# Two decoder stacks in float32 on one core: the mixer's first steps in another order, and the latent attention's up-projections as three products of rounded halves

## The chip, the core and the metric

The kernel runs on one core of a Trainium2 chip. Its engines run side by side and wait for each other through semaphores: TensorE (PE, matrix products into PSUM; PEld are its weight loads), VectorE (DVE), ScalarE (ACT, functions from tables that have to be loaded), GpSimd (POOL) and SyncE (SP), which only issues transfers. The metric is the time of one execution on the device in microseconds. Less is better.

## The reference, cut to what matters

Two stacks of two layers each, batch 1, 256 tokens of width 1024, all float32. The first stack's layer is feed-forward, token mixer, feed-forward, each with a layer norm behind it. The second stack has a multi-head latent attention (MLA) and a gated linear attention (GLA), over 256 tokens and 256 context tokens. The change touches the head of the token mixer and the latent attention:

```python
def token_mixer(h, w_in, w_out, gdn_conv, ...):
    qkv_a, a_a, b_a, z_a, qkv_b, qk_c, v_c, i_c, f_c, o_c = jnp.split(h @ w_in, IN_SPLITS, axis=-1)
    qa, ka, va = jnp.split(causal_conv_silu(qkv_a, gdn_conv), 3, axis=-1)
    qa = l2norm(split_heads(qa).astype(f32))
    ka = l2norm(split_heads(ka).astype(f32))
    ...
    beta = jax.nn.sigmoid(b_a.astype(f32))
    oa = gated_delta_rule(qa, ka, va, g.transpose(0, 2, 1), beta.transpose(0, 2, 1)).transpose(0, 2, 1, 3)
    ...

def mla_mixer(hc, hx, row, col, w_in, q_norm_g, w_uq, kv_norm_g, w_ukv, w_out):
    def project(h, rotate):
        cq, ckv, kr, gate = split_last(h @ w_in, (MLA_Q_RANK, MLA_KV_RANK, MLA_ROPE, MLA_WIDTH))
        q = (rms_norm(cq, q_norm_g) @ w_uq).reshape(b, n, MLA_HEADS, MLA_NOPE + MLA_ROPE)
        kv = (rms_norm(ckv, kv_norm_g) @ w_ukv).reshape(b, n, MLA_HEADS, MLA_NOPE + MLA_V)
        ...
    ox = attention_blocks(qx, jnp.concatenate([kc, kx], axis=1), jnp.concatenate([vc, vx], axis=1))
```

MLA has 16 heads, the ranks are 384 for queries and 256 for keys and values, a head has 64 + 32 columns of query and key and 64 of value.

## The kernel before

**Products of halves.** A float32 product on TensorE is two instructions. Most large products are done otherwise: an operand x is split into hi, x rounded to the shorter format fp32r, and lo, x - hi, and a product is the sum of hi·hi, lo·hi and hi·lo, one instruction each. ScalarE writes the hi part of a weight chunk (a copy with a rounding), VectorE the lo part (a subtraction, below called a low).

**The ring.** All weights come from one stream of chunks of 128 x 2048 float32 (1 MB), which SyncE loads in order into 8 ring slots. A chunk may be loaded when the chunk 8 places before it is released. For most chunks of halves the hi part takes the next slot and the lo part is written over the chunk (`take_both`).

**The order of work** on each engine is the order in which the program is written; there is no scheduler. A mixer (`mixer(l)`, m = 1 and 4) begins with six projections on TensorE, chunks 12, 0, 1, 2, 3, 4 of `w_in` (`WIN_FIRST`), into PSUM banks 1 to 6. Chunk 12 gives a gate tile (tile 24, ScalarE, `gate_or_copy`) and the rows of decays (`r_u`, VectorE). Chunks 0 to 4 give tiles 0 to 8 of queries, keys and values of the delta rule, each through `conv` on VectorE (four instructions) and SiLU on ScalarE, and gate tile 9. After the fifth projection TensorE needs the squares of tiles 0 to 5 (`l2sq`) for the sums `blk` x `g_sq`, six float32 products (`wk,tab`, twelve instructions), then goes on with the sixth projection, with fills (`fill(n)` takes the next items of a list of independent work, `BESIDE`: products p6.0, p6.1, p7.0, ...), with the transposed rows, the products key x key and key x query (`kk`, `qk`), and p13. VectorE does between these the lows of the chunks to come (`win_low`), `rows()` (running sums of decays), the normalised queries and keys, `g_kb` and `g_vb` (keys and values times beta), the mask on the decays (`gb_read`) and low 8.

In the layer norm ahead of a mixer ScalarE writes the normed tokens also into `res` (`affine(..., "normed")`, eight instructions), VectorE waits for these before the mixer, and also for ScalarE's reading of the gate tile (`proj_read_a`).

**The latent attention** (`mla()`, m = 6). The input stage makes 14 units of 128 columns from 7 chunks `mla_in`; units 0 to 4 are the latents `cq` (3 tiles of queries' and 2 of keys' latents, 512 tokens wide), which are normalised on VectorE once their sums are there (`cqr`, `cqn`). Between the last units stand `keys_values(0, 0..3)` and `queries(0)`, `queries(1)`. The sixteen heads follow. In head h TensorE does `scores(h)`, `turned(h-1)` (12 transposes), `queries(h+2)`, in even heads `weighted(h//2-1)`, and below head 12 `keys_values(h//4+1, h%4)`. VectorE does `maxima(h)` (L2594, L2595), the copy of part of the turned scores, in heads 12 to 14 a low of the output weights, `normalise(h)`, a copy of half the keys where h%4 < 2, `q_part(h+2)` (rotation of the query), `out_part` in even heads and `heads_low` in odd ones. ScalarE does the exponentials of `h` between maxima and normalise, and copies. `queries` and `keys_values` are plain float32 products on `cq`: 48 of 512 columns for the queries; 16 of 512 and 32 of 256 for keys and values. Their weights are 4 chunks `uq` (4 heads each) and 2 chunks `ukv` (8 heads each). VectorE also computes the modulation vectors of GLA there (`mod_part`, `LATE_MODS`), two halves of a chunk each.

Of the kernel before, what the change touches and what calls it, by code (L numbers as in the profile page):

```python
# [10 lines left out]
F32 = mybir.dt.float32  # L11
# [79 lines left out]
def build(nc, stream, cond_in, cols_in, tab_in, wg_in, xt_in, ct_in, out, spread, marks):  # L91
# [3 lines left out]
    with ExitStack() as ctx:  # L95
# [22 lines left out]
        assert nc.sbuf_base == wk_at + 4 * WK  # L118
        cond = sb("cond", [P, D])
        mod = sb("mod", [P, 4, 48])  # L120
# [10 lines left out]
        x2lo = nc.alloc_sbuf_tensor_at("x2lo", [P, KT, 2 * T], F32R, offset=wk_at + 4 * NEW)  # L131
# [98 lines left out]
        r_u, r_ab, r_ln = [g_at[:, 256 * i:256 * i + 256] for i in range(3)]  # L230
# [62 lines left out]

        def tree_bank(li):

            return 7 if li % 2 == 0 else 6
# [6 lines left out]
        LATE_AT = {2: (0,), 3: (1, 2), 4: (3, 4), 5: (5,), 6: (6, 7)}  # L303
# [37 lines left out]
        def _(eng):  # L341
# [156 lines left out]
            def mixer(l):  # L498
# [140 lines left out]
                for i, ch in enumerate(WIN_FIRST):  # L639
# [19 lines left out]
                for p in range(3, 6):  # L659
                    eng.wait_ge(*step_of("proj_read", m, p))  # L660
# [6 lines left out]
                eng.wait_ge(vector_done, step("kb", m))  # L667
                eng.wait_ge(vector_done, step("gb_read", m))
# [10 lines left out]
                eng.wait_ge(scalar_done, step("ekd", m))  # L679
# [158 lines left out]
            def mla():  # L838
# [51 lines left out]
                def keys_values(g, i):  # L890

                    w, b = state["ukv"], bank(6)
                    if i < 2:
                        for k in range(2):
                            at = 256 * (g % 2) + P * i
                            mm(b, w[:, k, at:at + P], cq[:, 3 + k, :], k == 0, k == 1)
                    else:
                        for t in range(2):
                            for k in range(2):
                                at = P * (2 * i - 4 + t)  # L900
                                mm(b[:, 256 * t:256 * t + 256], cq[:, 3 + k, at:at + P], w[:, k, 512 + 256 * (g % 2):768 + 256 * (g % 2)], k == 0, k == 1)
                    if g % 2 and i == 3:
# [7 lines left out]
                def next_keys(j):  # L910

                    state["ukv"] = tiles(take("ukv", j), D)
                    state["ukv_no"] = held[0]
# [7 lines left out]
                def queries(h):  # L921

                    if h % 4 == 0:
                        state["uq"] = take("uq", h // 4)[:, 0:1536].rearrange("p (k n) -> p k n", k=3)
                        state["uq_no"] = held[0]
                    w, hh = state["uq"], h % 4
                    if h == 0:
                        eng.wait_ge(*step_of("in2_read", m, 8))
                    elif h == 1:
                        eng.wait_ge(*step_of("in2_read", m, 12))  # L930
                    else:
                        eng.wait_ge(vector_done, step("q_read", h - 1))
                    for k in range(3):
                        mm(bank(0 if h else 2), w[:, k, P * hh:P * hh + P], cq[:, k, :], k == 0, k == 2)
                    if hh == 3:
# [92 lines left out]
                for i in range(3, 7):  # L1028
# [4 lines left out]
                    if i == 5:  # L1033
                        next_keys(0)
                    for n in (2 * i, 2 * i + 1):
# [15 lines left out]
                        if n >= 10:  # L1051
                            if n == 10:
                                eng.wait_ge(scalar_done, step("cqe", 1))
                                eng.wait_ge(vector_done, step("cqn", m))
# [39 lines left out]
                for h in range(MLA_H + 1):  # L1094
# [17 lines left out]
                    if h < 12:  # L1112
                        if h == 4:
                            next_keys(1)
# [339 lines left out]
        def _(eng):  # L1454
# [90 lines left out]
            def norm(m):  # L1545
# [34 lines left out]
                for c in range(2, 4):  # L1580
                    if to_ffn:
                        whole(m + 1, c)
                    else:
                        win_high(m + 1, c)
                g0_, b0_ = COLS["ln_g"][0] + 8 * m, COLS["ln_b"][0] + 8 * m
                affine(m, res[:, :, XS], tiles(ff_cen, 256), cols[:, g0_:g0_ + 8], cols[:, b0_:b0_ + 8], range(0, 4))
                eng.wait_ge(vector_done, step("xn", m, 3))
# [1433 lines left out]
```

## Time and profile before

| | us |
|---|---|
| median of three runs | 1775.43 |
| lowest, highest | 1773.72, 1776.09 |
| the profiled execution | 1776.33 |
| its span | 1774.3 |
| TensorE busy | 1686.1 |
| VectorE busy | 1323.5 |
| ScalarE busy | 777.0 |

The profile is of one execution. The span runs from the first to the last instruction. A busy TensorE is not one at its peak, since its instructions overlap: the time that a product costs is the distance from one start to the next, not the duration of one. Idle time of an engine counts only where others wait for it.

### The profile page before, as it was taken

The page shows a single profiled execution, that of the slowest core. Times are in us where ns is not written, and L with a number is a line of the kernel's source. Part 1 is how long each engine was busy: PE and PEld are TensorE (multiplying, and loading weights), DVE is VectorE, ACT ScalarE, POOL GpSimd, SP SyncE. Part 2 cuts the span into 40 slices and gives each one's busy share as a digit, 9 for nine tenths or more (in the row PEclk, how much of TensorE's full clock was granted, in tenths as well). Part 3 has the DMA queues.
Part 4 walks back from the last instruction along what each step waited for, and adds up shares of the span by engine and source line. Part 5 has one row for each costly group of instructions (what it writes and reads, how often), then busy time and mean ns, then how long its engine had stood idle before and what let it go on. Part 6 is the DMA issues. An engine that isn't in the chain of part 4 may idle for free. (4 is left out here: it accounts for less than half of the span.)

```text
span 1774.3 us, 30736 instructions
## 1 busy us (share of the span) xinstructions
PE 1686.1 (95%) x13112; PEld 1512.1 (85%) x13112; DVE 1323.5 (75%) x1965; ACT 777.0 (44%) x997; POOL 6.3 (0%) x14
## 2 busy tenths in 40 slices
PE   2999989999999999999899999999999999999998
PEld 2999978888899989999798779999886555759898
DVE  7777788855877778998878557999767768567844
ACT  2433365323633354343753327343652345355354
POOL 0000000000000000000000000000000000000000
PEclk9999999999999999999999999999999999999999
DMA  9868536351577746885364435776153200223102
GB/s 390 340 270 305 207 108 246 133 202 63 203 305 285 282 180 271 321 316 198 119 227 155 179 128 207 273 279 229 48 213 143 95 34 15 107 95 143 48 24 96
DMA packets 48807, 331.92 MB, mean 187 GB/s; under 512 B 5256, under 2 KB 8480, under 8 KB 9376
## 3 DMA queue, kind: packets, MB, share of 16 engines
q1 hardware_dynamic: 47808, 326.79, 48.2%
q0 software_dynamic: 864, 3.17, 0.7%
q8 instruction: 104, 1.70, 0.4%
q14 instruction: 31, 0.25, 0.0%
HBM read 328.87 MB, written 1.07 MB: 186 GB/s over the span
## 5 line engine op out<-in xcount | busy, mean ns | idle before, releaser
L347 PE MATMUL ps<-xhi,low 128*128 128x256 f32 x2048 | 499.5, 283 | 4.2 <-ACT xhi L1459 4.2
L347 PEld LDWEIGHTS ps<-xhi,low 128*128 128x128 f32 x2048 | 360.5, 190 | 6.4 <-ACT xhi L1459 5.6
L347 PE MATMUL ps<-xhi,whi_wk 128*128 128x256 f32 x1072 | 298.5, 288 | 40.5 <-ACT xhi L1459 38.7
L347 PE MATMUL ps<-xlo,whi_wk 128*128 128x256 f32 x1072 | 291.5, 281 | 0.0
L1459 ACT ACTIVATE wk<-ps 128x256 f32<-128x256 f32 (+5 forms) x219 | 108.1, 503 | 386.8 <-PE ps L347 320.8
L1459 ACT ACTIVATE whi_wk<-ring 128x2048 fp32r<-128x2048 f32 x100 | 191.6, 1918 | 195.3 <-DMA ring<-in_stream_dram 145.2
L347 PEld LDWEIGHTS ps<-xhi,whi_wk 128*128 128x128 f32 x1072 | 203.5, 195 | 43.2 <-issue 41.8
L2068 DVE TENSOR_TENSOR low<-ring,whi_wk 128x2048 fp32r<-128x2048 f32 (+1 forms) x101 | 228.4, 2264 | 6.6 <-ACT whi_wk L1459 6.6
L347 PE MATMUL ps<-wk 64*64 64x64 f32 (+10 forms) x2712 | 210.3, 262 | 5.8 <-ACT wk L1459 4.3
L347 PEld LDWEIGHTS ps<-wk 64*64 64x64 f32 (+4 forms) x2712 | 162.3, 146 | 55.0 <-issue 29.5
L347 PEld LDWEIGHTS ps<-xlo,whi_wk 128*128 128x128 f32 x1072 | 197.9, 189 | 0.0
L347 PE MATMUL ps<-hhi,low 128*128 128x256 f32 x704 | 196.8, 280 | 0.0
L2083 DVE CUSTOM_DVE_ANT_0 ring<-ring,cond,cols 128x1024 f32<-128x1024 f32 x144 | 178.3, 1278 | 11.0 <-DMA cols<-in_cols_dram 10.9
L1459 ACT ACTIVATE wk<-wk 128x256 f32<-128x256 f32 (+9 forms) x154 | 94.6, 643 | 200.9 <-DVE wk L2074 154.9
L347 PE MATMUL ps<-xa,ring 128*128 128x256 f32 (+1 forms) x608 | 146.0, 396 | 3.4 <-DVE xa L2071 3.1
L2068 DVE TENSOR_TENSOR wk<-wk,ps 128x256 f32<-128x256 f32 (+2 forms) x130 | 57.9, 462 | 122.1 <-ACT wk L1459 108.6
L347 PE MATMUL ps<-hhi,whi_wk 128*128 128x256 f32 x528 | 148.0, 280 | 0.0
L347 PE MATMUL ps<-hlo,whi_wk 128*128 128x256 f32 x528 | 147.9, 280 | 0.0
L347 PEld LDWEIGHTS ps<-xa,ring 128*128 128x128 f32 x608 | 114.3, 191 | 30.1 <-issue 11.5
L347 PEld LDWEIGHTS ps<-hhi,low 128*128 128x128 f32 x704 | 132.2, 188 | 0.0
L2068 DVE TENSOR_TENSOR low<-ring,low 128x2048 fp32r<-128x2048 f32 x41 | 93.2, 2286 | 48.4 <-ACT low L1459 48.2
L347 PE MATMUL ps<-wk,tab 128*128 128x256 f32 (+3 forms) x370 | 96.6, 422 | 22.8 <-ACT wk L1459 19.9
(141 smaller groups left out, 2861.7 us busy)
## 6 DMA issues: line engine op xcount, KB each, us to landing
ring<-in_stream_dram SPq DMA_DIRECT2D x302, 1024.0 KB, 5.7
ring<-in_cond_dram SPq DMA_DIRECT2D x4, 1024.0 KB, 4.6
wk<-spread_dram POOLq DMA_DIRECT2D x4, 384.0 KB, 5.1
wk<-spread_dram POOLq DMA_DIRECT2D x2, 768.0 KB, 6.9
tab<-in_tab_dram SPq DMA_DIRECT2D x1, 1440.0 KB, 20.5
res<-in_xt_dram SPq DMA_DIRECT2D x1, 1024.0 KB, 17.5
res<-in_ct_dram SPq DMA_DIRECT2D x1, 1024.0 KB, 9.9
out_dram<-wk SPq DMA_DIRECT2D x4, 256.0 KB, 2.4
```

Source lines behind the costliest of these rows:

```text
L347: last[0] = nc.tensor.matmul(o, l, r, start=start, stop=stop, skip_group_check=free)
L1459: return nc.scalar.activation(o, i, f, **kw)
L2068: return do(v.tensor_tensor(o, a, b, op), *key)
L2083: return do(v.tensor_tensor_reduce(o, w, c, 1.0, bias, MUL, ADD, total), *key)
```

## The change

**In the mixers.** ScalarE no longer writes `res` in the layer norm ahead of a mixer but in two halves inside it, behind SiLU of tiles 1 and 3, and reads the gate tile of chunk 12 only after the exponentials and logarithm of the rows. VectorE waits for neither. Low 5 moves from behind tiles 2 and 3 to behind tile 5, ahead of `rows()`. Tile 8's convolution moves from before low 7 to behind `g_kb`; `kk` on TensorE and the decays on ScalarE then wait for `g_kb` only, and `kk` no longer for the mask on the decays. The two fills on ScalarE stand apart. `r_u` and its neighbours have other places in memory.

**In the latent attention.** `queries` and `keys_values` become three products of halves each. The latents are split once: five roundings on ScalarE (`cqh`), five lows on VectorE (`cql`), and one of them is copied later (`cqh_later`). The weights come in 8 chunks of 768 columns (2 heads each) and 4 of 1024 (4 heads each), each in a whole ring load; both halves stay in its slot (`half_places`), rounded by `up_high` and subtracted by `up_low`. One modulation vector moves behind the last chunk `mla_in` (`LATE_AT`).

In the diff a line of "..." marks what is left out.

```diff
@@ tables
-        LATE_AT = {2: (0,), 3: (1, 2), 4: (3, 4), 5: (5,), 6: (6, 7)}
+        LATE_AT = {2: (0,), 3: (1, 2), 4: (3,), 5: (4,), 6: (5, 6, 7)}
+        UP_SIZE = {"uq": 768, "ukv": 1024}
+        def half_places(n, size):
+            return low[:, n % RING, D:D + size], low[:, n % RING, 0:size]
@@ TensorE, mixer
+                        eng.wait_ge(scalar_done, step("proj_read_a", m, 0))
                         eng.wait_ge(scalar_done, step("l2sq", m))
...
-                for p in range(3, 6):
-                    eng.wait_ge(*step_of("proj_read", m, p))
...
-                eng.wait_ge(vector_done, step("kb", m))
-                eng.wait_ge(vector_done, step("gb_read", m))
+                eng.wait_ge(vector_done, step("kbk", m))
...
-                eng.wait_ge(scalar_done, step("ekd", m))
+                for p in range(3, 6):
+                    eng.wait_ge(*step_of("proj_read", m, p))
+                eng.wait_ge(scalar_done, step("proj_read_a", m, 5))
@@ TensorE, latent attention
                         for k in range(2):
-                            mm(b, w[:, k, at:at + P], cq[:, 3 + k, :], k == 0, k == 1)
+                            mm(b, hi[:, k, at], cq_hi(3 + k), k == 0, False)
+                            mm(b, lo[:, k, at], cq_hi(3 + k), False, False)
+                            mm(b, hi[:, k, at], cq_lo[:, 3 + k, :], False, k == 1)
...
+                def up_halves(kind, i, n):
+                    take(kind, i)
+                    eng.wait_ge(vector_done, step("ulow", kind, i))
+                    return [tiles(p, n) for p in half_places(held[0], UP_SIZE[kind])]
...
                     for k in range(3):
-                        mm(bank(0 if h else 2), w[:, k, P * hh:P * hh + P], cq[:, k, :], k == 0, k == 2)
+                        mm(o, hi[:, k, at], cq_hi(k, h), k == 0, False)
+                        mm(o, lo[:, k, at], cq_hi(k, h), False, False)
+                        mm(o, hi[:, k, at], cq_lo[:, k, :], False, k == 2)
...
-                        if h == 4:
-                            next_keys(1)
+                        if h % 4 == 0:
+                            next_keys(h // 4 + 1)
@@ ScalarE, mixer
-                eng.wait_ge(tensor_done, step("proj", m, 0))
-                gate_or_copy(24, bank(1, 0, 256), "proj_read_a", m, 0)
...
                 win_high(m, 4)
+                eng.wait_ge(vector_done, step("proj_read", m, 0))
+                gate_or_copy(24, bank(1, 0, 256), "proj_read_a", m, 0)
                 for t in range(6):
                     silu(t)
-                    if t == 1:
-                        win_high(m, 5)
-                    if t == 3:
-                        win_high(m, 6)
+                    if t in (1, 3):
+                        win_high(m, 5 + t // 2)
+                        normed(m - 1, t // 2)
@@ ScalarE, latent attention
                 root(rs2, "cqr", m)
+                for t in (3, 4, 0, 1, 2):
+                    eng.wait_ge(vector_done, step("cqn", t))
+                    act(cq_hi(t), cq[:, t], ACT.Copy, "cqh", t).then_inc(scalar_done, 1)
...
+                        up_high(("ukv", "uq")[(n - 7) // 2], 0)
...
+                up_high("uq", 1)
+                up_high("ukv", 1)
...
+                    if h % 2 and h < 12:
+                        up_high("uq", h // 2 + 2)
+                    if h in (2, 6):
+                        up_high("ukv", h // 4 + 2)
@@ VectorE, norm and mixer
-                eng.wait_ge(scalar_done, step("normed", m))
+                if m % 3:
+                    eng.wait_ge(scalar_done, step("normed", m))
...
-                    if ch in (12, 4):
-                        eng.wait_ge(scalar_done, step("proj_read_a", m, i))
...
-                    if ch < 2:
-                        win_low(m, 4 + ch)
+                    if ch == 0:
+                        win_low(m, 4)
                     if ch == 2:
+                        win_low(m, 5)
                         rows()
                         win_low(m, 6)
...
+                tt(g_kb, qkv[:, 3:6], tiles(g_pair[:, 0:768], 256), MUL, "kbk", m).then_inc(vector_done, 1)
+                eng.wait_ge(scalar_done, step("proj_read_a", m, 5))
+                conv(8, bank(6, 0, 256), "proj_read", m, 5)
@@ VectorE, latent attention
+                eng.wait_ge(vector_done, done.count)
+                for t in (3, 4, 0, 1, 2):
+                    eng.wait_ge(scalar_done, step("cqh", t))
+                    tt(cq_lo[:, t], cq[:, t], cq_hi(t).bitcast(F32), SUB, "cql", t).then_inc(vector_done, 1)
+                def up_low(kind, i):
+                    n, size = found["chunk_no", kind, i][1], UP_SIZE[kind]
+                    hi, lo = half_places(n, size)
+                    eng.wait_ge(scalar_done, step("uround", kind, i))
+                    tt(lo, ring[:, n % RING, 0:size], hi.bitcast(F32), SUB, "ulow", kind, i).then_inc(vector_done, 1)
...
+                up_low("uq", 1)
                 q_part(1)
+                copy(cqh_later[:, :], cqh_first[:, :].bitcast(F32), "cqh_later").then_inc(vector_done, 1)
+                up_low("ukv", 1)
                 modulation(7)
...
+                    if h % 2 and h < 12:
+                        up_low("uq", h // 2 + 2)
+                    if h in (2, 6):
+                        up_low("ukv", h // 4 + 2)
```

Where the rows come to stand, at three places. First ScalarE at the start of the first mixer, before the change, from the roundings of chunks 2 and 3 (`low<-ring`) on; `res<-wk,cols` are the eight writes, `res<-ps` is the gate tile:

```order
L1459 ACTIVATE low<-ring 128x2048 x2
L1459 ACTIVATE res<-wk,cols 128x256 x8
L1459 ACT_TABLE_LOAD
L1459 ACTIVATE res<-ps 128x256
L1459 ACT_TABLE_LOAD
L1459 ACTIVATE wk<-wk 128x256
L1459 ACTIVATE wk<-wk 32x256
L1459 ACTIVATE small<-cols 128x1
L1459 ACT_TABLE_LOAD
L1459 ACTIVATE wk<-wk 128x256
L1459 ACTIVATE low<-ring 128x2048
L1459 ACT_TABLE_LOAD
```

And after it:

```order
L1491 ACTIVATE low<-ring 128x2048 x2
L1491 ACTIVATE wk<-wk 128x256
L1491 ACTIVATE wk<-wk 32x256
L1491 ACTIVATE small<-cols 128x1
L1491 ACTIVATE wk<-wk 128x256
L1491 ACTIVATE low<-ring 128x2048
L1491 ACT_TABLE_LOAD
L1491 ACTIVATE res<-ps 128x256
L1491 ACT_TABLE_LOAD
L1491 ACTIVATE wk<-wk 128x256 x2
L1491 ACTIVATE low<-ring 128x2048
L1491 ACTIVATE res<-wk,cols 128x256 x4
```

The eight writes have moved in two halves behind later roundings (the second half comes four rows further on), the gate tile behind the rows' functions, and two of four table loads are gone.

Second, VectorE in the first mixer, from the end of tile 3's convolution to the first row of the row work (`wk<-wk 128x256`); a convolution is a TENSOR_SCALAR and three rows behind it, `low<-ring,low` is the low of a weight chunk. Before:

```order
L2074 SCALAR_TENSOR_TENSOR wk<-ps,cols,wk 128x254
L2074 SCALAR_TENSOR_TENSOR wk<-ps,cols,wk 128x253
L2068 TENSOR_TENSOR low<-ring,low 128x2048
L2071 TENSOR_SCALAR wk<-ps,cols 128x256
L2074 SCALAR_TENSOR_TENSOR wk<-ps,cols,wk 128x255
L2074 SCALAR_TENSOR_TENSOR wk<-ps,cols,wk 128x254
L2074 SCALAR_TENSOR_TENSOR wk<-ps,cols,wk 128x253
L2071 TENSOR_SCALAR wk<-ps,cols 128x256
L2074 SCALAR_TENSOR_TENSOR wk<-ps,cols,wk 128x255
L2074 SCALAR_TENSOR_TENSOR wk<-ps,cols,wk 128x254
L2074 SCALAR_TENSOR_TENSOR wk<-ps,cols,wk 128x253
L2074 SCALAR_TENSOR_TENSOR wk<-wk 128x256
```

After:

```order
L2129 SCALAR_TENSOR_TENSOR wk<-ps,cols,wk 128x254
L2129 SCALAR_TENSOR_TENSOR wk<-ps,cols,wk 128x253
L2126 TENSOR_SCALAR wk<-ps,cols 128x256
L2129 SCALAR_TENSOR_TENSOR wk<-ps,cols,wk 128x255
L2129 SCALAR_TENSOR_TENSOR wk<-ps,cols,wk 128x254
L2129 SCALAR_TENSOR_TENSOR wk<-ps,cols,wk 128x253
L2126 TENSOR_SCALAR wk<-ps,cols 128x256
L2129 SCALAR_TENSOR_TENSOR wk<-ps,cols,wk 128x255
L2129 SCALAR_TENSOR_TENSOR wk<-ps,cols,wk 128x254
L2129 SCALAR_TENSOR_TENSOR wk<-ps,cols,wk 128x253
L2123 TENSOR_TENSOR low<-ring,low 128x2048
L2129 SCALAR_TENSOR_TENSOR wk<-wk 128x256
```

Low 5 stood ahead of the convolutions of tiles 4 and 5 and now stands behind them, ahead of the row work.

Third, VectorE in head 3 of the latent attention, from the copy of the turned scores to the maxima of head 4 (`whi_xa<-xa,o_hi` is `heads_low`). Before:

```order
L2077 COPY wk<-ps 128x512
L2603 RECIPROCAL small<-small 128x4
L2071 TENSOR_SCALAR wk<-wk,small 128x256 x2
L2071 TENSOR_SCALAR wk<-wk,small 128x512 x2
L2068 TENSOR_TENSOR wk<-ps,tab 96x512
L2068 TENSOR_TENSOR tab<-ps,tab 32x512
L2068 TENSOR_TENSOR wk<-wk,tab 32x512
L2068 TENSOR_TENSOR whi_xa<-xa,o_hi 128x512
L2594 TENSOR_REDUCE small<-ps 128x2
```

After:

```order
L2132 COPY wk<-ps 128x512
L2674 RECIPROCAL small<-small 128x4
L2126 TENSOR_SCALAR wk<-wk,small 128x256 x2
L2126 TENSOR_SCALAR wk<-wk,small 128x512 x2
L2123 TENSOR_TENSOR wk<-ps,tab 96x512
L2123 TENSOR_TENSOR tab<-ps,tab 32x512
L2123 TENSOR_TENSOR wk<-wk,tab 32x512
L2123 TENSOR_TENSOR whi_xa<-xa,o_hi 128x512
L2123 TENSOR_TENSOR low<-ring,low 128x768
L2665 TENSOR_REDUCE small<-ps 128x2
```

There is one row more, the low of a `uq` chunk, ahead of the next head's maxima. So it is in every odd head below 12; heads 2 and 6 get one of 128x1024 (`ukv`) in the same place.

## Rows read from the trace of the kernel before

**Rows 1.** The page, part 1: busy time and share of the span.
```profile
PE 1686.1 (95%) x13112; PEld 1512.1 (85%) x13112; DVE 1323.5 (75%) x1965; ACT 777.0 (44%) x997; POOL 6.3 (0%) x14
```

**Rows 2.** Windows: length, busy PE, PEld, DVE, ACT, POOL; granted clock, DMA share, GB/s.
```profile
262.00:270.00 8.00, 2.76 (x20) 2.50 (x19) 7.32 (x18) 4.18 (x5) 0.00 (x0) 0.85 0.46 156
270.00:275.00 5.00, 5.00 (x16) 4.01 (x15) 4.80 (x7) 0.74 (x2) 0.70 (x2) 0.55 0.01 3
```

**Rows 3.** Timeline, PE: start, duration, instruction [idle before <-releaser]; the two mixers.
```profile
269.32 5.38 PE L347 MATMUL ps<-wk,tab 128*128 128x256 f32 x12 [5.24 <-ACT wk L1459]
...
297.72 0.51 PE L347 MATMUL ps<-low,xhi 128*128 128x256 f32 x2
...
303.37 0.80 PE L347 MATMUL ps<-tab,wk 64*64 64x64 f32 x20
...
883.48 2.05 PE L347 MATMUL ps<-wk,tab 128*128 128x256 f32 x4 [5.24 <-ACT wk L1459]
```

**Rows 4.** Timeline, DVE, first mixer.
```profile
246.76 0.54 DVE L2071 TENSOR_SCALAR wk<-ps,cols 128x256 f32<-128x256 f32 x1 [3.64 <-ACT res L1459]
...
263.11 0.48 DVE L2071 TENSOR_SCALAR wk<-ps,cols 128x256 f32<-128x256 f32 x1
...
267.32 0.43 DVE L2074 SCALAR_TENSOR_TENSOR wk<-wk 128x256 f32<-128x256 f32 x1
...
274.03 2.29 DVE L2068 TENSOR_TENSOR low<-ring,low 128x2048 fp32r<-128x2048 f32 x1
...
283.35 2.28 DVE L2068 TENSOR_TENSOR low<-ring,low 128x2048 fp32r<-128x2048 f32 x1
...
294.05 2.29 DVE L2068 TENSOR_TENSOR low<-ring,low 128x2048 fp32r<-128x2048 f32 x1
```

**Rows 5.** Timeline, ACT, start of the first mixer.
```profile
240.90 4.03 ACT L1459 ACTIVATE res<-wk,cols 128x256 f32<-128x256 f32 x8
244.95 1.28 ACT L1459 ACT_TABLE_LOAD   x1
```

**Rows 6.** Timeline, PE, end of the latent attention's input stage.
```profile
...
1360.04 0.62 PE L347 MATMUL ps<-whi_xa,low 128*128 128x512 f32 x2
...
1360.74 0.63 PE L347 MATMUL ps<-whi_xa,low 128*128 128x512 f32 x2
...
1361.43 1.89 PE L347 MATMUL ps<-ring,wk 128*128 128x256 f32 x8
1363.16 2.74 PE L347 MATMUL ps<-wk,ring 128*128 128x512 f32 x6
1365.73 2.75 PE L347 MATMUL ps<-wk 96*128 96x256 f32 x8
```

**Rows 7.** Timeline, DVE, attention heads: scores' first maximum (L2594) of heads 4 to 8.
```profile
1406.36 0.69 DVE L2594 TENSOR_REDUCE small<-ps 128x2 f32<-128x512 f32 x1
...
1414.06 0.69 DVE L2077 COPY wk<-ps 64x512 f32<-64x512 f32 x1 [1.62 <-PE ps L347]
...
1417.65 0.68 DVE L2594 TENSOR_REDUCE small<-ps 128x2 f32<-128x512 f32 x1
...
1437.75 0.69 DVE L2594 TENSOR_REDUCE small<-ps 128x2 f32<-128x512 f32 x1 [1.23 <-PE ps L347]
...
1447.00 0.69 DVE L2594 TENSOR_REDUCE small<-ps 128x2 f32<-128x512 f32 x1
```

**Rows 8.** Timeline, DVE: two subtractions of 1024 columns, two products of 768.
```profile
1284.91 2.36 DVE L2068 TENSOR_TENSOR x2lo<-wk,whi_xa 128x1024 fp32r<-128x1024 f32 x2
...
288.01 1.82 DVE L2068 TENSOR_TENSOR wk<-wk 128x768 f32<-128x768 f32 x2
```

**Rows 9.** Timeline, PE, head 4: the weighted sum.
```profile
1409.29 2.81 PE L347 MATMUL ps<-wk 128*64 128x256 f32 x24
```

**Rows 10.** Timeline, DVE, just before the heads.
```profile
1365.93 0.69 DVE L2068 TENSOR_TENSOR wk<-ps,tab 96x512 f32<-96x512 f32 x1 [2.70 <-PE ps L347]
```

**Rows 11.** DMA issues of 235 to 290 us: KB each, median us to landing.
```profile
ring<-in_stream_dram SPq DMA_DIRECT2D x9, 1024.0 KB, 4.8
```

More of the change, by code:

```diff
@@ L229, in build @@
         g_t, g_tt, g_dt, g_at, g_att = [W(SCR + 1536 * i, 1536) for i in range(5)]
-        r_u, r_ab, r_ln = [g_at[:, 256 * i:256 * i + 256] for i in range(3)]
+        r_u, r_ab, r_ln = W(23040, 256), W(23296, 256), r_rw
         g_sq = g_t
@@ L292, in build, with cq_hi @@
         a_end, a_tot = small[:, 40:44], small[:, 44:48]
+        def cq_hi(t, h=0):
+            return cqh_q[:, t] if t < 2 else cqh_kv[:, t - 3] if t > 2 else cqh_later[:, :] if h > 1 else cqh_first[:, :]
+        def half_places(n, size):
+            return low[:, n % RING, D:D + size], low[:, n % RING, 0:size]
         def tree_bank(li):
@@ L1053, in mla @@
                                 eng.wait_ge(scalar_done, step("cqe", 1))
-                                eng.wait_ge(vector_done, step("cqn", m))
+                                eng.wait_ge(vector_done, step("cql", 4))
+                                next_keys(0)
                             else:
@@ L1584, in norm, with normed @@
                         win_high(m + 1, c)
+                if to_ffn:
+                    normed(m, 0)
+                    normed(m, 1)
+            def normed(m, part):
                 g0_, b0_ = COLS["ln_g"][0] + 8 * m, COLS["ln_b"][0] + 8 * m
-                affine(m, res[:, :, XS], tiles(ff_cen, 256), cols[:, g0_:g0_ + 8], cols[:, b0_:b0_ + 8], range(0, 4))
-                eng.wait_ge(vector_done, step("xn", m, 3))
-                affine(m, res[:, :, XS], tiles(ff_cen, 256), cols[:, g0_:g0_ + 8], cols[:, b0_:b0_ + 8], range(4, 8), "normed", m)
+                if part:
+                    eng.wait_ge(vector_done, step("xn", m, 3))
+                affine(m, res[:, :, XS], tiles(ff_cen, 256), cols[:, g0_:g0_ + 8], cols[:, b0_:b0_ + 8], range(4 * part, 4 * part + 4),
+                       *(("normed", m) if part else ()))
             def ffn(l, f):
@@ L1711, in mixer @@
                 gate_or_copy(9, bank(6, 256, 512), "proj_read_a", m, 5)
+                fill(1)
                 silu(6)
                 silu(7)
+                fill(1)
+                win_high(m, 8)
                 silu(8)
-                win_high(m, 8)
-                fill(2)
                 eng.wait_ge(pairs_in, 32 * (l + 1))
-                eng.wait_ge(vector_done, step("kb", m))
+                eng.wait_ge(vector_done, step("kbk", m))
                 cs = tiles(g_pair[:, 768:1536], 256)
@@ L1874, in mla, with up_high @@
                     act(tiles(sq2, 512)[:, t], res[:, t, :], ACT.Square, "sq7", t).then_inc(scalar_done, 1)
+            def up_high(kind, i):
+                n, size = found["chunk_no", kind, i][1], UP_SIZE[kind]
+                eng.wait_ge(landed[n % RING], loads(n))
+                act(half_places(n, size)[0], ring[:, n % RING, 0:size], ACT.Copy, "uround", kind, i).then_inc(scalar_done, 1)
             def high(*tag):
@@ L2971, in chunk_of @@
     if kind == "ukv":
-        heads = range(8 * tag[1], 8 * tag[1] + 8)
+        heads = range(4 * tag[1], 4 * tag[1] + 4)
         return columns(a["mla_w_ukv_2"][0], [(128 * h, 64) for h in heads] + [(128 * h + 64, 64) for h in heads], 2)
@@ L2975, in chunk_of @@
         s = []
-        for h in range(4 * tag[1], 4 * tag[1] + 4):
+        for h in range(2 * tag[1], 2 * tag[1] + 2):
             s += [(96 * h, 96)] + [(96 * h + 64 + p, 8) for p in [8, 0, 24, 16]]
```

54 lines of the change are left out of this document (34 added, 20 removed).

## The prediction

> **What bounds the kernel now.** I read the page's busy shares first, then TensorE's idle times in the timeline, then, at each of them, the engine it waits for. TensorE is busy 95% of the span [rows 1], so only two things can shorten the program: TensorE's waits, and TensorE's work where nothing else sets the pace. The longest wait of a mixer is the one before the sums of squares (`wk,tab` x12): 5.24 us, in both mixers [rows 3]. It costs more than itself. In the window with it the granted clock falls, and in the next five microseconds it is 0.55 of full, half speed (1.2 GHz) for nearly all of it [rows 2]; the twelve sums take 4.9 us from 269.32 to 274.22, about twice the 2.45 of full speed. From there to the end of the mixer TensorE has no wait of 0.3 us: fills cover it.
>
> In the 16 attention heads it is different. From head to head I follow VectorE's first maximum (L2594). Heads 4 to 7 take 40.64 us [rows 7], and in them VectorE idles 1.62 and 1.23 us on TensorE; else it waits only for the exponentials, some 1.9 us a head, which follow its own maxima. So a chain through VectorE and ScalarE sets the pace of most heads, and TensorE that of a few.
>
> **The mixers, step by step** (the first; the second is built alike). TensorE ends its fifth projection at 264.1 (269.32 - 5.24). One projection is 48 products of halves; 48 of them take 303.37 - 297.72 = 5.65 us [rows 3], 0.118 each. What comes last before the sums is VectorE's sixth convolution, done at 267.3 [rows 4]. Its chain stood still for 3.64 us before 246.76, waiting for ScalarE: eight writes of `res` (4.03 us) and a table load (1.28) stood in front of the gate that VectorE waited for [rows 4, 5]. The change takes both out of VectorE's way: it begins at 243.1 (246.76 - 3.64), and from then on it is the projections that hold it. The fourth ends at 258.4, two convolutions take 267.32 - 263.11 = 4.2 [rows 4], so the sixth ends at 262.6: 4.7 earlier. SiLU and squares took 2.0 from there to the sums, so these begin near 264.7. The writes of `res` return in two halves of 2.0 us between ScalarE's SiLUs; by 4.8-us landings [rows 11] and 1.9-us roundings ScalarE too reaches the squares only at 262.9, so they just fit. TensorE waits 0.6 instead of 5.24, keeps its clock, and is done with the sums at 267.2 instead of 274.2: 7.0 ahead. `res` itself is read again only at the mixer's end, so its later writing holds up nobody.
>
> Not all of it stays. The next weights' lows are VectorE's, and that gained only 4.7. One low of 2.3 us now stands ahead of the row work, which begins at 264.9 and takes 274.03 - 267.32 = 6.7 [rows 4]; low 6 ends at 273.9. TensorE, with its sixth projection, is there at 272.9: a wait of 1.0. Low 7 follows two convolutions instead of three and ends at 280.4, TensorE comes at 279.9: 0.5. Then keys, 5.85 us of small products, and low 8. In the old trace low 8 ended at 296.34, 10.7 after low 7; the ninth convolution (2.1) has moved into this stretch, less a wait of 0.9 that it can fill: 292.3 to 293.2, I take 293.0. TensorE gets there at 292.0, so its next product begins at 293.0 against 297.72 [rows 3]: 4.7 earlier. Behind it, masks and decays on VectorE are 3.3 earlier and had 1.5 us of slack, which just covers the rest. Two mixers: **9.4 us less**, with 6 and 13 as ends (another 1.7 us lost on each; or nearly the whole 7.0 kept).
>
> **The latent attention.** TensorE's own saving is plain. A float32 product of 512 columns is two instructions of (1365.73 - 1363.16)/6 = 0.43 us, one of 256 two of (1363.16 - 1361.43)/8 = 0.216; three products of halves of 512 columns take 1360.74 - 1360.04 = 0.70 [rows 6], of 256 columns 0.353 [rows 3]. There are 64 and 32 of them: 128 x 0.43 + 64 x 0.216 = 68.8 us before, 64 x 0.70 + 32 x 0.353 = 56.1 after, 12.7 less. For that VectorE gets 5 lows of 512 columns, 8 of 768 and 4 of 1024 and a copy; ScalarE the roundings, which fit its idle time. The prices: 2.36/2 = 1.18 for 1024, 1.82/2 = 0.91 for 768 [rows 8].
>
> Of the loads, SyncE issues six more of 1 MB each (12 chunks of latent weights for 6), in a stretch where the queue stands idle for most of the time; their ring slots come free a head or more ahead of the roundings, but for one. Ahead of the heads TensorE gains 2.2 us: two queries of 0.47 less, four parts of keys and values of 0.33 less. VectorE had 2.70 us of idle time there [rows 10] and 4 more ahead of low 5, where the five new lows of the latents go. What remains on it after that are 1.18 + 0.91 + 0.91 + 1.18 us of weights' lows and 0.7 of the copy, 4.9, of which the idle times and an earlier landing of the last input weights take nearly all but the last. That last one, the low of key weights 1, is bound in another way: its ring slot comes free with the first group's values at 1361.4, 4.8 to landing [rows 11], 1.0 to round, 1.2 for the low, and the first maximum stands behind it on VectorE: 1369.1 against 1368.6. Cost **+0.5** (0 to +3).
>
> In the heads I take each by its kind. An odd head below 12 has the chain maxima, exponentials, scaling, query, low of the heads, and no wait on TensorE; a low of 768 columns comes behind it, in front of the next head's maxima: 0.91 and 0.05 of gap, six times, +5.8. What TensorE saves there hides nothing, since it already waited. In an even head the weighted sum starts 2.93 us behind the maxima (1409.29 - 1406.36 [rows 7, 9]), for VectorE's copy of the turned scores, so shorter queries don't move it; behind it the shorter keys give 0.33 in heads 4 and 8 (where VectorE waited 1.62 for them) and 0.43 in head 10. Heads 2 and 6 had 1.23 us of slack on VectorE and get a low of 1.18, +0.1 each. Heads 12 and 13 were set by VectorE's lows of the output weights and stay. Sum: 5.8 - 0.66 - 0.43 + 0.2 = **+4.9**. The part that was to gain 12.7 us loses 5.4. Its ends: -9 if TensorE's path counted after all, +9 if the lows cost VectorE their full price everywhere.
>
> The sum is -9.4 + 5.4 = -4.0 us. The profiled execution took 1776.33 us (span 1774.3 and 2.0 around it), so 1772.3; the median of the three runs is 0.9 lower, so 1771.4.
>
> One rule of the skill speaks against part of this. In the trace the table load takes 1.28 us and the next function follows at once [rows 5]. The Trainium skill (ScalarE: Activation LUTs, What ACT_TABLE_LOAD costs) puts 1.38 us of draining beside the load. With its figure the two loads ahead of the first SiLU would put ScalarE behind VectorE by some 2 us, each mixer would gain 3.4 instead of 4.7, and the sum would be -1.4; I go by the row.
>
> **Rivals.** (a) *TensorE sets the pace in the heads.* Its 95% speaks for it, the missing VectorE idle time in odd heads against. Whole: -9.4 - 12.7, 1753; in part, with the lows in time that VectorE idles anyway and the attention at no change: 1766. (b) *The mixer's wait only changes its name.* ScalarE's path to the squares ties with VectorE's; if a landing takes 7 us or the moved writes come in its way, TensorE waits 2.5 us more, and each mixer gains 2 to 2.5: -4.7 + 5.4, 1776. (c) *The half clock in the heads, slower.* TensorE's work per head falls from 9.6 to 8.8 us while the head gets longer, so it idles more often, up to 1.5 us at a time. If the clock falls as it did behind the mixer's wait, each fall costs up to 2.45 us [rows 3]; four falls turn the sum, six give +14.7 - 4.0, 1786. Against it: TensorE's idle times there stay well below 5.24. The Trainium skill (TensorE: Matmul & The Clock Gate, A second HAM failure mode: psum-queue depth-cycling) tells of a kernel whose clock swings between its two levels from frequent short idles alone; no run here shows that yet. (d) *The weights' lows come late ahead of the heads*, the first maximum by 3 us more and PE's queries behind them: 1775.
>
> **Chances.** Forecast 0.45 (own range 1768 to 1775); (a) 0.25, most of it near 1766; (b) 0.15; (c) 0.07; (d) 0.08. Range: 1761 to 1779, which leaves out (a) whole and (c). 0.2% is 3.6 us, about what a measurement of this kernel can tell from none. Faster by more: four fifths of the forecast and (a), 0.61; within: the rest of the forecast, most of (b) and of (d), 0.26; slower: (c) and what is left of (b) and (d), 0.13.
>
> **What would show it.** The mixers: TensorE's idle time before `wk,tab` x12 under 1.5 us and the clock at 1.00 behind it; instead waits near 1, 0.4 and 1 us for lows 6, 7 and 8; the first product of `low,xhi` in the first mixer at 293. The attention: from head 0's first maximum to head 12's 124 us instead of 119; VectorE without idle time on TensorE in odd heads, TensorE's waits on `low` from VectorE. I am wrong if the heads get shorter, if the clock in them is below 0.98, or if the squares on ScalarE start after 264.

## The result, and the profile after

| | us |
|---|---|
| before, median of four runs | 1774.78 |
| changed, median of four runs (1783.34 to 1786.53) | 1784.39 |
| ratio, 95% interval | 1.0057 (1.0045 to 1.0069) |
| changed, measured again (e12) | 1.0043 (1.0029 to 1.0056) |
| predicted | 1771.4 (1761 to 1779) |

The change made the kernel slower by 8 to 10 us; a gain of 4 was predicted. I follow TensorE through the changed kernel's trace, which is of the slowest of its four executions (1786.53 us). First its timeline in the two mixers (start, duration, instruction, idle before and releaser), which answers to [rows 3]:

```profile
264.73 2.83 PE L363 MATMUL ps<-wk,tab 128*128 128x256 f32 x12 [0.62 <-ACT wk L1491]
...
273.98 0.51 PE L363 MATMUL ps<-xhi,low 128*128 128x256 f32 x2 [0.78 <-DVE low L2123]
...
280.48 0.48 PE L363 MATMUL ps<-xhi,low 128*128 128x256 f32 x2 [0.35 <-DVE low L2123]
...
286.52 5.92 PE L363 MATMUL ps<-wk 64*128 64x128 f32 x48
295.66 0.77 PE L363 MATMUL ps<-low,xhi 128*128 128x256 f32 x2 [3.22 <-ACT wk L1491]
...
304.01 1.61 PE L363 MATMUL ps<-tab,wk 64*64 64x64 f32 x48
...
902.16 10.77 PE L363 MATMUL ps<-wk 64*128 64x128 f32 x48 [2.31 <-DVE wk L2123]
912.86 0.79 PE L363 MATMUL ps<-low,xhi 128*128 128x256 f32 x2
...
920.04 1.61 PE L363 MATMUL ps<-tab,wk 64*64 64x64 f32 x48
```

The wait before the sums went from 5.24 to 0.62 us, and the waits for lows 6 and 7 are the small ones forecast. TensorE is as far ahead as it should be until the keys' products. Then comes a wait that was not forecast: 3.22 us behind the keys' products in the first mixer, 2.31 ahead of them in the second. The windows of the changed kernel (length, busy times, granted clock, DMA share, GB/s) show what it drags along:

```profile
262.00:270.00 8.00, 7.38 (x53) 6.90 (x53) 7.47 (x17) 5.81 (x6) 0.00 (x0) 1.00 0.44 163
270.00:275.00 5.00, 4.22 (x36) 4.02 (x35) 4.83 (x4) 4.13 (x4) 1.75 (x3) 1.00 0.16 29
...
292.00:300.00 8.00, 4.78 (x24) 4.62 (x24) 7.70 (x10) 3.83 (x14) 0.00 (x0) 0.66 0.53 219
...
905.00:915.00 10.00, 9.88 (x47) 9.28 (x47) 9.63 (x11) 6.46 (x19) 0.00 (x0) 0.50 0.55 228
```

The clock of 0.85 and 0.55 around the sums [rows 2] is 1.00 now, but it falls to half speed (1.2 GHz) behind the new wait. In the second mixer the 48 small products take 10.70 us from start to start where they took 5.85. VectorE's timeline says who is late, in the first mixer and in the second:

```profile
285.43 0.17 DVE L2132 COPY small<-wk 128x3 f32<-128x3 f32 x1 [2.71 <-DMA wk<-spread_dram]
...
293.23 2.28 DVE L2123 TENSOR_TENSOR low<-ring,low 128x2048 fp32r<-128x2048 f32 x1
...
901.08 0.17 DVE L2132 COPY small<-wk 128x3 f32<-128x3 f32 x1 [4.87 <-DMA wk<-spread_dram]
...
908.88 2.29 DVE L2123 TENSOR_TENSOR low<-ring,low 128x2048 fp32r<-128x2048 f32 x1
```

VectorE stands 2.71 us until the spread rows (`g_pair`, loaded by GpSimd's queue) have landed, 4.87 in the second mixer, and low 8, for which TensorE waits, ends at 295.51 instead of near 293 (911.17 in the second). TensorE's row at 295.66 names ScalarE as the releaser: the last of twelve exponentials there ends within 0.1 us of low 8. But by the program this product waits for low 8 and for a copy of ScalarE that was done at 292.03. Why the rows are late is in the timelines of SyncE's and GpSimd's queues. The kernel before:

```profile
280.38 0.81 SPq L1432 DMA_DIRECT2D ring<-in_stream_dram  x2
...
276.83 1.35 POOL L2850 DMA_DIRECT2D wk<-spread_dram  x2 [1.34 <-DMA spread_dram<-wk]
```

The changed kernel:

```profile
273.24 0.80 SPq L1464 DMA_DIRECT2D ring<-in_stream_dram  x2
...
274.43 1.35 POOL L2928 DMA_DIRECT2D wk<-spread_dram  x2 [1.34 <-DMA spread_dram<-wk]
```

The DMA issues of 264 to 300 us (KB each, median us to landing), before:

```profile
wk<-spread_dram POOLq DMA_DIRECT2D x2, 384.0 KB, 5.1
wk<-spread_dram POOLq DMA_DIRECT2D x1, 768.0 KB, 6.9
```

and changed:

```profile
wk<-spread_dram POOLq DMA_DIRECT2D x2, 384.0 KB, 9.7
wk<-spread_dram POOLq DMA_DIRECT2D x1, 768.0 KB, 13.7
```

Two weight loads of 1 MB leave when the sixth projection has freed their slots. TensorE reaches that 7.1 us earlier; the rows, which hang on VectorE, leave only 2.4 earlier. So the order is reversed: the rows left 3.5 us ahead of the weights and now leave 1.2 us behind them. The DMA queues of the changed kernel in steps of two microseconds (packets, MB, share of the 16 engines' time; q1 carries weights, q0 rows), in turn from 275, 277 and 281 us:

```profile
q1 hardware_dynamic: 94, 0.77, 93.9%
...
q1 hardware_dynamic: 114, 0.80, 95.5%
q0 software_dynamic: 5, 0.02, 2.5%
...
q0 software_dynamic: 119, 0.42, 100.1%
```

Until 279 the weights have the engines nearly to themselves; then the rows pass, at half the weights' rate (0.42 MB in 2 us against 0.80).

In the heads, VectorE's first maxima of heads 0 and 12, which answer to [rows 7]:

```profile
1372.38 0.69 DVE L2665 TENSOR_REDUCE small<-ps 128x2 f32<-128x512 f32 x1
...
1496.92 0.69 DVE L2665 TENSOR_REDUCE small<-ps 128x2 f32<-128x512 f32 x1
```

TensorE in heads 0 and 2:

```profile
1376.94 5.46 PE L363 MATMUL ps<-wk 96*128 96x256 f32 x8 [3.27 <-ACT wk L1491]
...
1393.33 0.70 PE L363 MATMUL ps<-cqh_q,low 128*128 128x512 f32 x2 [1.46 <-DVE low L2123]
```

From head 0 to 12 it is 124.5 us (119.1 before; 124 was forecast). TensorE is 0.6 us behind before at the end of the first mixer, 2.7 at the start of the attention and 9.3 at its end. So in this execution the mixers cost 2.7 instead of giving 9.4, and the attention cost 6.6 instead of 5.4.

### The profile page after: what moved, and what is told of

It reads as the page before. It is cut to its first block and busy times, and to the rows that moved or that the text cites. A ratio compares the mean times of both kernels' runs of the same rounds, so it can differ in the third digit from the quotient of the medians.

```text
span 1783.6 us, 30974 instructions
## 1 busy us (share of the span) xinstructions
PE 1682.8 (94%) x13208; PEld 1530.7 (86%) x13208; DVE 1338.4 (75%) x1983; ACT 785.2 (44%) x1010; POOL 6.3 (0%) x14
## 5 line engine op out<-in xcount | busy, mean ns | idle before, releaser
L363 PE MATMUL ps<-wk 64*64 64x64 f32 (+10 forms) x2712 | 218.0, 266 | 13.5 <-ACT wk L1491 10.0
L363 PEld LDWEIGHTS ps<-wk 64*64 64x64 f32 (+4 forms) x2712 | 167.4, 149 | 59.0 <-issue 31.3
L2123 DVE TENSOR_TENSOR low<-ring,low 128x2048 fp32r<-128x2048 f32 (+2 forms) x53 | 105.6, 2004 | 44.1 <-ACT low L1491 43.9
L363 PE MATMUL ps<-whi_xa,low 128*128 128x256 f32 (+1 forms) x552 | 115.1, 332 | 1.9 <-ACT whi_xa L1491 1.9
## 6 DMA issues: line engine op xcount, KB each, us to landing
wk<-spread_dram POOLq DMA_DIRECT2D x4, 384.0 KB, 10.3
```

The costliest lines, as they stand in the source:

```text
L363: last[0] = nc.tensor.matmul(o, l, r, start=start, stop=stop, skip_group_check=free)
L2123: return do(v.tensor_tensor(o, a, b, op), *key)
```

## The experiments

All ratios are to the kernel before on the same chip, with 95% intervals; 0.001 is 1.8 us. e1 to e4 and e12 ran on one chip, e5 to e11 on another.

**e1, e2, e12: the parts.** e1 has the hunks in the mixers and layer norms alone, e2 all others, e12 is the changed kernel.

> The kernel before with the mixers' part of the change alone. Theory 1 (collision): in the changed kernel two loads of weights leave SyncE's queue at 273.24, 1.2 us ahead of the loads of the spread rows (274.43), where before they left at 280.38, 3.5 us behind them; the rows land late, VectorE stands 2.71 us, TensorE 3.22 us, and the clock falls behind that. Then this kernel is slower than before by about the 2.7 us that the changed kernel is behind at the start of the latent attention: 1777 to 1778. Rival (the prediction's sum holds for the mixers and the loss lies in the interplay with the attention): 1765, faster by 9.4.

> The kernel before with the latent attention's part alone. By the two traces the attention costs 6.6 us (from 2.7 behind at its start to 9.3 at its end): 1781.4. The prediction's sum gave 5.4: 1780.2. If the parts aren't additive (the attention's loads or clock suffer from the mixers), 1775 or less.

> The changed kernel once more, in as many rounds as its parts. The parts alone gave ratios of 1.0006 (mixers) and 1.0032 (attention), together 1.0038; the change gave 1.0057 in fewer runs. If the parts are independent, this comes out near 1.004 (7 us); if they make each other worse (more falls of the clock, or the longer run of loads), near 1.0057 again (10 us).

Measured: e1 1.0006 (0.9997 to 1.0015), e2 1.0032 (1.0020 to 1.0045), e12 1.0043 (1.0029 to 1.0056). The parts add up to 1.0038, inside e12's interval; the first measurement of the change (1.0057, 1.0045 to 1.0069) lies above it. The mixers' part alone is worth nothing, neither the 9.4 of the sum nor clearly a loss, and e1's trace has nearly the waits of the changed kernel's (2.79 and 2.05 us, where that has 3.22 and 2.31). The attention costs 5.7.

**e3, e5, e9: rows first.** SyncE holds back the two loads until the mixer's rows are there; nothing else changes (`hold` lists the first load of each mixer into a slot that the sixth projection frees). e3 is the changed kernel with it, e5 the mixers' part, e9 the kernel before.

```diff
                 if n >= RING:
                     eng.wait_ge(*step_of("chunk", n - RING))
+                for l in range(DEPTH):
+                    if n == hold[l]:
+                        eng.wait_ge(pairs_in, 32 * (l + 1))
```

> The changed kernel, but SyncE waits, before the two loads of weights that the sixth projection frees, until the spread rows of that mixer have landed. Theory 1: rows land in 5 to 7 us as before, VectorE's wait of 2.71 is gone, TensorE's 3.22 and 2.31 too, low,xhi begins near 293.0 and the clock stays up: each mixer gets its 4.7 us, together 12.1 from 1784.4: 1772.3. Rival 2 (the rows are late for another reason, or the order of VectorE's work, keys ahead of the ninth convolution and low 8 last, sets the end anyway): low,xhi stays at 295 or later, 1780 to 1785. Rival 3 (the loads held back come late themselves): new waits for ring in the mixers, over 1785.

> The mixers' part alone (e1), with SyncE waiting for the spread rows as in e3. e3 made the mixers worth about 8.7 us with the attention's part in place (1782.3 of e2 less 1773.65). If collision and attention are independent: ratio to before near 0.995, 1767.8. If the attention's part hid something of it: 1771 or more.

> A control: the kernel before with nothing but SyncE's wait for the spread rows. In its trace the rows' loads leave 3.5 us ahead of the weights' and land before VectorE wants them (285.1 against 287.9). Theory 1: there is no collision to take away, so nothing changes: within 2 us of before. Rival (the wait helps a mixer in itself, or the weights' loads held back come late): more than 3 us faster or slower.

Measured: e3 0.9983 (0.9972 to 0.9993), e5 0.9942 (0.9928 to 0.9956), e9 1.0003 (0.9995 to 1.0012). The DMA issues of e3's first mixer:

```profile
wk<-spread_dram POOLq DMA_DIRECT2D x2, 384.0 KB, 5.8
wk<-spread_dram POOLq DMA_DIRECT2D x1, 768.0 KB, 7.5
```

Its timeline, VectorE's copy and TensorE's next product:

```profile
281.98 0.16 DVE L2137 COPY small<-wk 128x3 f32<-128x3 f32 x1
...
292.20 0.47 PE L363 MATMUL ps<-low,xhi 128*128 128x256 f32 x2 [0.64 <-ACT wk L1496]
```

VectorE waits no more, TensorE 0.64 instead of 3.22. One wait on SyncE's queue is worth 0.0060 in the changed kernel (against e12) and 0.0064 in the mixers' part, 11 us for two mixers, and nothing in the kernel before, where rows left first anyway. So it does not help in itself; it takes back the collision that the change made. Its rivals 2 and 3 fall: the new order of VectorE's work is no hindrance, and the weights held back come in time. With it the mixers' part alone gains 10.3 us, near the 9.4 of the prediction.

**e8: a weaker hold.** The same edit with `rows_stored` in place of `pairs_in`, so that both kinds of load leave together.

> As e3, but SyncE waits only until the rows are stored, so that its two loads of weights leave at the same time as the loads of the spread rows. Theory 1a (what counts is which is queued first at the DMA engines): the rows have 1.35 us of issuing on GpSimd's queue, and the first load of 1 MB still gets ahead of part of them: landings 7 to 9 us, part of the gain, 1776 to 1779. Theory 1b (bandwidth is shared, order doesn't matter): landings of 9 to 10 us as in the changed kernel, 1783. If 5 to 7 us as in e3: 1773.7.

Measured: 1.0051 (1.0039 to 1.0063), no better than the change. The queues' timeline in its first mixer:

```profile
272.72 0.80 SPq L1469 DMA_DIRECT2D ring<-in_stream_dram  x2
...
272.92 1.35 POOL L2933 DMA_DIRECT2D wk<-spread_dram  x2 [1.35 <-DMA spread_dram<-wk]
```

Its DMA issues there:

```profile
wk<-spread_dram POOLq DMA_DIRECT2D x2, 384.0 KB, 10.4
wk<-spread_dram POOLq DMA_DIRECT2D x1, 768.0 KB, 15.9
```

The wait held the weights back by 1.0 us: they leave 9.5 us behind the start of the sums, 8.5 in the changed kernel. They are still 0.2 us ahead of the rows, for which GpSimd's queue needs 1.35 us to issue. So a lead of 0.2 us instead of 1.2 brought the rows' landing nothing (10.4 and 15.9 against 9.7 and 13.7). The result lies near 1b's forecast (9 to 10 us, 1783) and misses 1a's (7 to 9 us, 1776 to 1779). That order doesn't matter at all is not shown by it: in e3 it did, and no kernel here let the rows go first by a fraction of a microsecond. What e8 shows is that leaving together is not enough. The Trainium skill (DMA: Bandwidth & Descriptors, Queues, rings and completion order) says that each DMA engine goes round the queues that have work, a packet at a time. The changed kernel's trace shows sharing only from 279 on (75% and 34% of the time in 279 to 281); in the two microseconds before, the rows' queue had 2.5%.

**e10: the wait and the clock apart.** The changed kernel, rows late, but TensorE fills its waits with products that nobody reads (in the second mixer also six of the keys' products again).

```diff
                 fill(2)
+                for i in range(12):
+                    mm(bank(2, 0, 256), blk, tiles(g_sq, 256)[:, i % 6], True, True)
                 eng.wait_ge(vector_done, step("kbk", m))
...
```

> The changed kernel, rows late as they are, but TensorE fills its waits with products that nobody reads: twelve sums of squares again ahead of the keys' products (about 2.8 us), and in the second mixer six of the keys' products again (1.5 us). This parts the late rows' cost into the wait and the half clock behind it. Theory: the clock stays at full speed from 290 to 303 and from 903 to 916, the first product of low,xhi comes when the last low allows (295.5; about 911), and the clock's share of 2.7 us in the first mixer and 3.1 in the second comes back: 5 to 6 us faster than the changed kernel, near 1780 where that has 1785 to 1786 and before 1776.5. Rival (the clock doesn't hang on the wait, or the filling itself costs): no faster than the changed kernel.

Measured: 1.0027 (1.0018 to 1.0037), against 1.0043 of e12. Windows in both mixers:

```profile
290.00:296.00 6.00, 5.89 (x50) 5.28 (x49) 5.80 (x8) 4.04 (x14) 0.00 (x0) 1.00 0.78 322
...
905.00:912.00 7.00, 6.89 (x61) 6.38 (x60) 6.80 (x8) 4.66 (x17) 0.00 (x0) 1.00 0.64 265
```

In the first mixer TensorE's filling (x24 is twelve float32 products), the first product of `low,xhi`, and VectorE's low 8:

```profile
284.83 5.34 PE L363 MATMUL ps<-wk,tab 128*128 128x256 f32 x24
...
295.96 0.51 PE L363 MATMUL ps<-low,xhi 128*128 128x256 f32 x2
...
291.45 2.29 DVE L2126 TENSOR_TENSOR low<-ring,low 128x2048 fp32r<-128x2048 f32 x1
```

The clock stayed up in both places. But the run does not part the wait from the clock as it was meant to. Its filling was planned at 2.8 us and takes 5.3, so TensorE comes too late for low 8: low 8 ends at 293.74 and the product starts at 295.96, 2.2 us behind it; in the second mixer it is 2.0 (911.38 against 909.36). In time, e10 is 0.0016 below e12, 2.8 us, less than the 5 to 6 expected; the intervals overlap and leave anything from none to nearly 6.

The traces part the two better. In the first mixer low 8 ends 31.4 us behind the end of the fifth projection in the changed kernel, 31.0 in e10, and 28.6 in e5: the lateness itself costs 2.8 us there. In the second mixer it is 33.6 in the changed kernel and again 28.6 in e5, 5.0 us. The clock comes on top of it (see below).

**e4, e11: the attention's lows elsewhere.** e4 is e2 with the lows of the weights behind the maxima, where VectorE waits for the exponentials, and their roundings a head earlier. e11 also puts the low of key weights 1 from ahead of the loop behind the first maxima (the lines with `h == 0`; the hunk of ScalarE is left out).

```diff
-                up_low("ukv", 1)
...
                     if h < MLA_H:
                         maxima(h)
+                    if h == 0:
+                        up_low("ukv", 1)
                     if h:
                         pt_copy(h - 1)
+                    if h % 2 and h < 12:
+                        up_low("uq", h // 2 + 2)
+                    if h in (2, 6):
+                        up_low("ukv", h // 4 + 2)
                     if 12 <= h < 15:
                         out_low(h - 12)
...
                         heads_low((h - 3) // 2)
-                    if h % 2 and h < 12:
-                        up_low("uq", h // 2 + 2)
-                    if h in (2, 6):
-                        up_low("ukv", h // 4 + 2)
```

> The attention's part alone as in e2, but the lows of the query and key weights stand behind the maxima of a head, where VectorE waits 1.8 to 2.6 us for the exponentials, and their roundings on ScalarE a head earlier. Theory (VectorE's and ScalarE's chain sets the pace of the heads, and a low costs only where it stands in the chain): six odd heads lose 0.96 each and TensorE's waits of 1.3 to 2.1 for low are gone: 1781.4 - 5.8 = 1775.6, at best 1 to 2 less since the shorter products now count in the even heads. Rival (the roundings or the landings now come in the way, or TensorE's clock is what costs): 1780 to 1783.

> The attention's part alone with lows behind the maxima and the key weights' low behind the first maxima: is it worth having without the mixers? e7 less e5 says 4.6 us faster than before; e4 (2.4 slower) less the 3 to 4 that the clock kept in the first heads gave in e7's sum says 1 to 2 faster. In the trace, heads 0 to 12 at 117.5 us instead of 119.1, no fall of the clock in 1370 to 1380.

Measured: e4 1.0007 (0.9998 to 1.0016), 4.4 us better than e2 where 5.8 was expected; e11 0.9985 (0.9976 to 0.9993), faster than before. Heads 0 to 12 take 124.5 us in e2, 119.2 in e4, 117.5 in e11. The same lows cost 5.3 us more behind the heads' last step than behind the maxima, where heads 0 to 12 take what they took before: VectorE's place in the chain, not its busy time, was the price. What e4 does not get rid of stands in its last heads:

```profile
1502.47 4.51 PE L363 MATMUL ps<-wk 96*128 96x256 f32 x8 [1.89 <-ACT wk L1491]
```

A wait of 1.89 us, and half speed behind it (4.51 for eight products that take 2.8); in the kernel before the clock is 1.00 there.

**e6, e7: everything together.** e6 is e3 with e4's edit, e7 with e11's too.

> Both remedies on the changed kernel: rows first (e3) and lows behind the maxima (e4). If their gains add, 3.4 us below e3: 1770.2, still 2.4 above e5, which has no attention part. If the clock falls again in the last heads as in e4 (a wait of 1.89 us and half speed behind it), no more than that; if it doesn't, 1768.5.

> e6, and the low of the second key weights stands behind the first head's maxima instead of ahead of them. Ahead of them it costs VectorE 0.8 of waiting for ScalarE (a late landing) and 1.23 of work, and TensorE then waits 3.2 us for the first exponentials and runs at half speed behind that (the next eight products take 5.46 instead of 2.8 us). Theory: first maxima 2.0 earlier, TensorE's wait split and the clock kept: 3 to 4 below e6, 1766.5. Rival: the wait only moves to the keys that need this low, and the clock falls there: 1770.

Measured: e6 0.9948 (0.9937 to 0.9960), e7 0.9915 (0.9903 to 0.9927): 15 us faster than before, the best of all. TensorE at head 0 in e6:

```profile
1360.45 5.46 PE L363 MATMUL ps<-wk 96*128 96x256 f32 x8 [3.20 <-ACT wk L1496]
```

In e7 TensorE waits instead where the program needs the low of key weights 1:

```profile
1357.76 0.70 PE L363 MATMUL ps<-cqh_kv,low 128*128 128x512 f32 x2 [1.21 <-issue]
```

The window of 1360 to 1365 in e6:

```profile
1360.00:1365.00 5.00, 4.55 (x8) 2.67 (x9) 4.34 (x9) 1.50 (x4) 0.00 (x0) 0.50 1.02 424
```

and in e7:

```profile
1360.00:1365.00 5.00, 4.66 (x24) 3.17 (x23) 4.74 (x8) 1.78 (x3) 0.00 (x0) 1.00 1.02 431
```

One wait of 3.20 has become 1.21, the clock stays up, and head 0 takes 9.1 us again instead of 10.1. By the ratios the step is worth 5.9 us, by the two traces 2.6; a part of it is that e6's executions differ among themselves (below).

## Why the prediction was wrong

**The mixers, as far as low 7: right.** A wait of 0.6 was forecast (0.62 and 0.61), sums done at 267.2 (267.21), clock kept there, waits of 1.0 and 0.5 for lows 6 and 7 (0.78 and 0.35), the squares in time. In the changed trace, too, the next function starts 0.02 us behind a table load. The 1.38 us of draining that the Trainium skill puts beside a load (ScalarE: Activation LUTs, What ACT_TABLE_LOAD costs), which by the prediction's estimate would have cost each mixer 1.3, did not show.

**The step that failed** is "low 8 ... I take 293.0" and, with it, "TensorE gets there at 292.0, so its next product begins at 293.0". The working counted VectorE's own instructions and left out that one of them needs the rows from GpSimd's queue. In the old trace the two loads that VectorE's copy at 287.94 waits for landed near 282.6 (the second left about 277.5, 5.1 to landing), and the third at 285.1, so no row showed a wait. I moved VectorE's demand 5 us forward and TensorE's release of two ring slots 7, and let the rows keep pace without looking at what lay ahead of them. Without the collision the step is right: 28.9 us from the fifth projection to that product were forecast, e5 has 28.8 in both mixers.

**The second missing term** is the clock behind the new wait. The prediction counted on keeping it because the old wait went. In the changed trace it is lost behind the new one. In the first mixer that costs 2.7 us (8.35 for the products up to the small ones that took 5.65). In the second, the keys' products take 4.85 us longer, but TensorE would have waited for low 8 until 911.17 anyway; it starts at 912.86, so 1.7 of them count, and 1.5 behind that: 3.2. Together the late rows cost some 8 us in this trace (2.8 and 5.0) and the clock some 6. e12 shows the spread: the same kernel kept the clock in the second mixer's keys' products, lost it behind the next wait, and its traced execution is 7.5 us faster (1779.03). In e10, with the waits filled, the clock stayed up in both mixers; that is one traced execution.

**The attention: right in mechanism, near in size.** +5.4 forecast, +6.6 in the trace, 5.7 by e2. TensorE's saving of 12.7 us gained nothing, odd heads paid for their lows, TensorE waited for `low` from VectorE instead. Two terms were off. The first maximum came 1.1 us later instead of 0.5. Of this 0.4 arose ahead of the changed part (TensorE is 3.1 us behind at 1307.98, not 2.7). The rest is 0.7: the last weights landed 5.1 us behind their slot instead of 4.8, the load leaving 0.2 behind it and taking 4.9. And the heads' +4.9 came out as +5.5 with other parts: heads 2 to 11 cost 2.8, less than forecast; heads 0 and 1 cost 2.7, of which 1.0 is a low. TensorE waited 3.27 us for the first exponentials and lost the clock for the next eight products. That is one of the falls of rival (c).

**The rivals.** (b), that the mixer's wait only changes its name, comes nearest, and had 0.15. Its title holds, its mechanism doesn't: it was worked out for ScalarE's path in front of the sums, with half of the gain left; the wait came 20 us further on, for rows from another queue, and took all. No rival had that. (c) had its mechanism in one place of the heads. (a) is out as it was put: shorter products brought nothing with the lows in the chain (e2), and a gain, of 2.7 us, only once VectorE's lows stood in its waits (e11). (d) was in the forecast's spread (0.6 more). The Trainium skill (TensorE: Matmul & The Clock Gate, A second HAM failure mode: psum-queue depth-cycling) tells of a clock that swings from short idles. The trace is against it here: in 1400 to 1490 of the changed kernel TensorE idles 10 of 90 us, in pieces up to 2.1, and the clock is 1.00.

## What to carry to other kernels

Before a step is moved forward, list the transfers that end in it and those that a faster engine sets off, with issue and landing of each: a transfer that landed 5 us early shows no wait and may still be the next bound. Where the order of two queues decides, make it explicit with a wait on the less urgent one; that was worth 11 us here. Work that goes to the engine in the chain costs its full time behind the last step of the chain, and here cost nothing that could be seen in the place where that engine waits for its answer. And before a wait is filled with idle work, price the filling by its instructions: here it took twice what was planned.

## What the hardware showed beside that

**Large loads ahead of small ones.** Two weight loads of 1 MB, issued 1.2 us ahead, moved the landing of 384 KB from 5.1 to 9.7 us and of 768 KB from 6.9 to 13.7; with the loads held back (e3) it was 5.8 and 7.5.

**The clock does not hang on the wait before it alone.** In e12 the second mixer's keys' products follow a wait of 1.90 and keep full speed; behind the 3.22 that comes next the clock is at half:

```profile
899.96 5.92 PE L363 MATMUL ps<-wk 64*128 64x128 f32 x48 [1.90 <-DVE wk L2123]
...
909.10 0.77 PE L363 MATMUL ps<-low,xhi 128*128 128x256 f32 x2 [3.22 <-ACT wk L1491]
```

With 2.31 in the changed kernel's first trace they took 10.77, and in e4 a wait of 1.89 was enough. In e3 the first mixer's products ran at half speed from 292.67, behind a wait of 0.64; e5, e6 and e7 had the same wait there and full speed. And the same kernel spreads over several microseconds together with its mean granted clock: e3's fastest execution took 1768.6 us at 0.993, its slowest 1776.9 at 0.987. What decides in these cases stays open.
